# Identity matmuls in TensorE's waits, routing weights applied at the evictions, a rearranged last stage and swapped PSUM bank pairs, in a one-layer attention, retention and mixture-of-experts kernel

## What is computed

```python
mix = jnp.einsum('bse,ed->bsd', mixed, w_out)                    # mixed: 512 x 1024
h_res = h_res + gate1 * _rms_norm(mix, g_post_mix)
h2 = _rms_norm(h_res, g_pre_ffn) * (1.0 + scale2) + shift2
# router: 4 groups, best one; 8 experts in it, best two
g_prob = softmax(t @ w_group + b_group);  g_top, g_sel = top_k(g_prob, 1)
e_top, e_sel = top_k(softmax(e_logits of that group), 2)
weights = g_top * e_top / sum(e_top)
for e in range(32):
    hid = silu(t @ w_gate_exp[e]) * (t @ w_up_exp[e])            # 512 x 256
    y = y + combine[:, e:e + 1] * (hid @ w_down_exp[e])          # combine: weights at the chosen experts
h_res = h_res + gate2 * _rms_norm(y, g_post_ffn)
```

## Time and profile before

| what | value |
|---|---|
| median of 3 timed runs | 758.62 us (758.47 to 759.87) |
| the profiled execution | 759.44 us, span 757.4 us |
| PE busy | 640.0 us (85% of the span) |
| PE weight loads | 322.0 us (43%) |
| DVE busy | 375.3 us (50%) |
| ACT busy | 156.6 us (21%) |
| POOL busy | 79.6 us (11%) |
| mean granted TensorE clock | 0.937 of full speed |
| DMA | 171.75 MB, mean 227 GB/s |

### The profile page before, as it was taken

How to read it: one execution, slowest core, us unless ns; L and a number is a source line. 1 busy time by engine, 2 the same in 40 slices (tenths; PEclk the granted TensorE clock), 3 DMA queues, 4 the chain that set the end, 5 groups by cost and what they waited for, 6 DMA issues and landing times. The chain is left out here.

```text
span 757.4 us, 7042 instructions
## 1 busy us (share of the span) xinstructions
PE 640.0 (85%) x2446; PEld 322.0 (43%) x2446; DVE 375.3 (50%) x724; ACT 156.6 (21%) x333; POOL 79.6 (11%) x105
## 2 busy tenths in 40 slices
PE   0499999999999999999899954999786999979720
PEld 0465644444455555565544544334232444333200
DVE  5755356989876743258823247523121232212227
ACT  1420111233122222311222231022111122112112
POOL 0013211210111110000000001111111211200010
PEclk9999999999999999999999965999898999999975
DMA  9980806050506060430821093599999999999344
GB/s 327 384 325 15 298 20 223 17 206 7 216 1 222 1 223 0 170 89 0 332 112 56 28 391 154 213 419 419 421 422 420 421 404 386 419 419 417 138 169 169
DMA packets 50115, 171.75 MB, mean 227 GB/s; under 512 B 10016, under 2 KB 10016, under 8 KB 37152
## 3 DMA queue, kind: packets, MB, share of 16 engines
q1 hardware_dynamic: 41808, 154.98, 52.8%
q0 software_dynamic: 5888, 10.52, 3.7%
q10 hardware_dynamic: 2384, 5.80, 2.0%
HBM read 168.13 MB, written 13.63 MB: 240 GB/s over the span
## 5 line engine op out<-in xcount | busy, mean ns | idle before, releaser
L619 PE MATMUL psum<-ring,hT 128*128 128x512 f32 (+1 forms) x576 | 234.8, 561 | 0.0
L619 PEld LDWEIGHTS psum<-ring,hT 128*128 128x128 f32 x576 | 102.8, 191 | 119.3 <-issue 119.0
L869 PE MATMUL psum<-ring,hT 128*64 128x512 f32 (+1 forms) x416 | 127.1, 631 | 16.7 <-issue 16.7
L869 PEld LDWEIGHTS psum<-ring,hT 128*64 128x64 f32 (+1 forms) x416 | 43.2, 151 | 87.4 <-issue 87.3
L1551 DVE TENSOR_SCALAR work<-work 128x256 f32<-128x256 f32 x18 | 5.3, 294 | 137.2 <-PE psum L879 110.2
L895 PE MATMUL psum<-ring,work 128*64 128x512 f32 (+1 forms) x208 | 64.7, 626 | 8.4 <-issue 7.0
L753 PE MATMUL psum<-ring,hT 128*128 128x512 f32 x128 | 57.5, 608 | 2.7 <-DVE ring L1425 2.0
L1170 DVE SCALAR_TENSOR_TENSOR rows<-ring,sm,rows 128x512 f32<-128x512 f32 x64 | 51.1, 799 | 1.7
L869 PE MATMUL psum<-rows,hT 128*64 128x512 f32 (+1 forms) x96 | 42.5, 595 | 1.3 <-issue 1.3
L1077 ACT ACTIVATE work<-psum 128x256 f32<-128x256 f32 x18 | 6.9, 384 | 170.8 <-PE psum L869 170.8
L1230 DVE TENSOR_TENSOR ropebuf<-psum,cosT 128x512 f32<-128x512 f32 (+1 forms) x24 | 14.7, 614 | 51.6 <-PE psum L619 39.4
(11 more groups left out here) (240 smaller groups left out, 715.7 us busy)
## 6 DMA issues: line engine op xcount, KB each, us to landing
ring<-in_w_gate_exp SPq DMA_DIRECT2D x26, 1024.0 KB, 13.0
ring<-in_w_up_exp SPq DMA_DIRECT2D x26, 1024.0 KB, 20.4
ring<-in_w_down_exp SPq DMA_DIRECT2D x26, 1024.0 KB, 21.9
ring<-in_w_in SPq DMA_DIRECT2D x8, 2048.0 KB, 9.3
ring<-in_w_ada SPq DMA_DIRECT2D x8, 2048.0 KB, 14.3
ring<-in_w_ada SPq DMA_DIRECT2D x8, 1024.0 KB, 14.0
rows<-in_w_gate_exp SPq DMA_DIRECT2D x6, 1024.0 KB, 14.6
rows<-in_w_up_exp SPq DMA_DIRECT2D x6, 1024.0 KB, 21.3
```

The source lines that it names most:

```text
L619: mm = pe.matmul(o[:, 0:width], hT3[:, k, b * P:(b + 1) * P], w[:, k, :], start=(k == 0), stop=(k == KD - 1))
L869: mm = pe.matmul(o[rows, :], XT[u % 2][:, k, rows], both(SLOT_OF[place])[:, k, :, :], start=(k == 0), stop=(k == KD - 1))
```

## The change

Four things. (1) The bank pairs of `wout` are swapped: blocks 0 and 2 use banks 6 and 7, blocks 1 and 3 banks 0 and 1. (2) PE gets `stream(n)`, n matmuls of the identity with 512 columns of the constants into bank 6, which nobody reads: 3 behind `route(2)`, 6 behind `route(3)`, 3 behind the rank matmuls, 5 behind the first rows' table. (3) The routing weights go through the table of the late rows (`IN_WT`, 34 more columns) into `row_wt`, a column for each unit, and the evictions of the units multiply by it. (4) In the tail DVE adds the two rows, multiplies by G2 while ACT works, and ends with one instruction for reciprocal root and residual; ACT loads its square root's table ahead of `y_base`.

```diff
-            use(("wout", b), (0, 6)[b % 2], 2)
+            use(("wout", b), (6, 0)[b % 2], 2)
...
+            def stream(n):
+
+                o = ps[6]
+                for _ in range(n):
+                    pe.matmul(o[:, :], ident, cst[:, 0:512], start=True, stop=True)
...
                     if 2 <= b <= NB:
                         route(b - 2)
+                    if b == NB:
+                        pe.wait_ge(mix_n, NB - 1)
+                        stream(3)
                     if 1 <= b <= NB:
                         turn_h2(b - 1)
                 route(NB - 1)
+                stream(6)
...
+                stream(3)
                 pe.wait_ge(early_ready, 1)
...
                 mm.then_inc(early_done, 1)
+                stream(5)
...
-                    mm = pe.matmul(o[:, 0:NT], IN_ROW[:, n, :], IN_TILE[:, n, :], start=(n == 0),
+                    mm = pe.matmul(o[:, 0:2 * NT], IN_ROW[:, n, :], IN_BOTH[:, n, :, :], start=(n == 0),
...
-                a.activation(YO[u % 2][:, 0:512], ps[Y_BANK[(2 * u) % 3]][:, :], ACT.Copy).then_inc(y_evA, 1)
+                if u == 0:
+                    act.wait_ge(wt_ready, 1)
+                a.activation(YO[u % 2][:, 0:512], ps[Y_BANK[(2 * u) % 3]][:, :], ACT.Identity, bias=zero,
+                             scale=row_wt[:, u:u + 1]).then_inc(y_evA, 1)
...
+            a.activation(yr, eps.to_broadcast([P, NB]), ACT.Sqrt, bias=eps).then_inc(tail_root, 1)
+            act.wait_ge(tail_root, 1)
             act.wait_ge(y_base, 1)
...
-                v.tensor_tensor(wts[:, :, 1:2], wts[:, :, 0:1], P2, ALU.mult)
+                link(v.tensor_tensor(wts[:, :, 1:2], wts[:, :, 0:1], P2, ALU.mult))
...
+                v.tensor_tensor(IN_WT, IN_TILE, in_pairs(wts, NT), ALU.mult)
...
                 dve.wait_ge(table_done, 1)
+                v.tensor_copy(row_wt, bank(("table",))[:, NT:2 * NT]).then_inc(wt_ready, 1)
...
-                v.tensor_copy(YO[u % 2][:, 512:1024], ps[Y_BANK[(2 * u + 1) % 3]][:, :]).then_inc(y_evV, 1)
+                v.tensor_scalar(YO[u % 2][:, 512:1024], ps[Y_BANK[(2 * u + 1) % 3]][:, :], row_wt[:, u:u + 1], None,
+                                ALU.mult).then_inc(y_evV, 1)
...
+            def combine(b):
+                y = YG[b]
+                dve.wait_ge(y_back[b], 16)
+                relay(v.tensor_tensor(y[:, 0, :], y[:, 0, :], y[:, 1, :], ALU.add), y_sum, b + 1)
+
+            def weigh(b):
+                y = YG[b]
+                v.tensor_tensor(y[:, 1, :], y[:, 0, :], G2, ALU.mult)
+
+            def finish(b):
+                y = YG[b]
+                dve.wait_ge(y_sq, b + 1)
+                link(v.reciprocal(yss[:, b:b + 1], yr[:, b:b + 1]))
+                v.scalar_tensor_tensor(out=y[:, 1, :], in0=y[:, 1, :], scalar=yss[:, b:b + 1], in1=x3[:, b, :],
+                                       op0=ALU.mult, op1=ALU.add).then_inc(o_add, 1)
+
+            combine(0)
+            weigh(0)
+            for b in range(NB):
+                if b + 1 < NB:
+                    combine(b + 1)
+                finish(b)
+                if b + 1 < NB:
+                    weigh(b + 1)
```

More of the change, by code:

```diff
@@ L322, in build @@
         yss, yr = cols(238, 4), cols(242, 4)
+        over_wt = cols(246, 1)
         top8 = cols(248, 8)
@@ L365, in build @@
         y_out = [sem("y_out0"), sem("y_out1")]
-        yw_ready, y_ss, y_sq, o_add = sem("yw_ready"), sem("y_ss"), sem("y_sq"), sem("o_add")
+        y_ss, y_sq, o_add = sem("y_ss"), sem("y_sq"), sem("o_add")
         y_back = [sem(f"y_back{b}") for b in range(NB)]
@@ L379, in build @@
         y_base = sem("y_base")
+        wt_ready, y_sum, tail_root = sem("wt_ready"), sem("y_sum"), sem("tail_root")
         h2_dram = nc.dram_tensor("h2_rows", [S, D], F32, kind="Internal").ap()
@@ L524, in build @@
         IN_ROW = ropebuf[:, 0:2 * NB * P].rearrange("p (n c) -> p n c", n=2 * NB)
-        IN_TILE = ropebuf[:, 1024:1024 + 2 * NB * NT].rearrange("p (n t) -> p n t", n=2 * NB)
+        IN_BOTH = ropebuf[:, 1024:1024 + 4 * NB * NT].rearrange("p (n w t) -> p n w t", n=2 * NB, w=2)
+        IN_TILE, IN_WT = IN_BOTH[:, :, 0, :], IN_BOTH[:, :, 1, :]
+        row_wt = retbuf[:, 1408:1408 + NT]
         CUM = retbuf[:, 1344:1472].rearrange("p (b n) -> p b n", b=NB)
@@ L1113, in overflow @@
                 act.wait_ge(ov_y, o + 1)
-                a.activation(YO[0][:, 0:512], ps[6][:, :], ACT.Copy).then_inc(ov_evA, 1)
+                act.wait_ge(ov_ix, o * 3 + 3)
+                a.activation(YO[0][:, 0:512], ps[6][:, :], ACT.Identity, bias=zero, scale=over_wt).then_inc(ov_evA, 1)
             act.wait_ge(y_out[0], 16 * (NU // 2))
             each_overflow(act, overflow)
+            a.activation(yr, eps.to_broadcast([P, NB]), ACT.Sqrt, bias=eps).then_inc(tail_root, 1)
+            act.wait_ge(tail_root, 1)
             act.wait_ge(y_base, 1)
@@ L1123, in _ @@
             for b in range(NB):
-                act.wait_ge(yw_ready, b + 1)
+                act.wait_ge(y_sum, b + 1)
                 a.activation(JUNK2, YG[b][:, 0, :], ACT.Square, accum_out=yss[:, b:b + 1]).then_inc(y_ss, 1)
@@ L1581, in overflow @@
                 dve.wait_ge(ov_y, o + 1)
-                v.tensor_copy(YO[0][:, 512:1024], ps[7][:, :]).then_inc(ov_evV, 1)
+                dve.wait_ge(ov_ix, o * 3 + 3)
+                v.tensor_scalar(YO[0][:, 512:1024], ps[7][:, :], over_wt, None, ALU.mult).then_inc(ov_evV, 1)
             dve.wait_ge(y_out[0], 16 * (NU // 2))
             each_overflow(dve, overflow)
-            for b in range(NB + 1):
-                if b < NB:
-                    y = YG[b]
-                    dve.wait_ge(y_back[b], 16)
-                    link(v.tensor_scalar(y[:, 1, :], y[:, 1, :], wts[:, b, 1:2], None, ALU.mult))
-                    relay(v.scalar_tensor_tensor(out=y[:, 0, :], in0=y[:, 0, :], scalar=wts[:, b, 0:1], in1=y[:, 1, :],
-                                                 op0=ALU.mult, op1=ALU.add), yw_ready, b + 1)
-                if b >= 1:
-                    q, y = b - 1, YG[b - 1]
-                    dve.wait_ge(y_sq, q + 1)
-                    link(v.reciprocal(yss[:, q:q + 1], yr[:, q:q + 1]))
-                    link(v.scalar_tensor_tensor(out=y[:, 1, :], in0=y[:, 0, :], scalar=yss[:, q:q + 1], in1=G2,
-                                                op0=ALU.mult, op1=ALU.mult))
-                    v.tensor_tensor(y[:, 1, :], y[:, 1, :], x3[:, q, :], ALU.add).then_inc(o_add, 1)
+            def combine(b):
[19 more added lines that the diff above has]
+                    weigh(b + 1)
         @block.gpsimd
@@ L1677, in overflow @@
                 g.tensor_copy(six[:, :], pid_t[:, bass.ds(o + NU, 1)]).then_inc(ov_ix, 1)
-                pool.wait_ge(ov_ix, o * 2 + 2)
+                g.tensor_copy(over_wt, row_wt[:, bass.ds(o + NU, 1)]).then_inc(ov_ix, 1)
+                pool.wait_ge(ov_ix, o * 3 + 3)
                 pool.sem_inc(pool_steps, 1)
```

## The result

| what | before | after |
|---|---|---|
| median | 759.01 us (758.47 to 759.87, 4 runs) | 745.39 us (744.92 to 746.14, 4 runs) |
| the profiled execution | 759.44 us, span 757.4 | 745.19 us, span 743.1 |
| PE busy | 640.0 us | 648.0 us |
| DVE busy | 375.3 us | 373.3 us |
| ACT busy | 156.6 us | 160.1 us |

The ratio is 0.9818 (95% interval 0.9805 to 0.9831): 13.6 us faster. The forecast was 748.4, 11.0 under the profiled execution of before; the measured median lies 0.2 under the lower end of the range, 745.6.

A forecast was written before the change was run, and what follows sets the result against it. TensorE was taken to bound the kernel through the output projection, then a routing chain of alternating engines, then full DMA engines, then VectorE's tail. Sum: 759.44-3.7-3.5-3.9=748.3, stated as 748.4, range 745.6 to 752.0.

The forecast's parts named there:

- Part 1, bank pairs: Output projection: swapped banks end a wait and a half-clock stretch, second half starts near 379.3; 3.7 us, bounds 2.0 and 3.7.
- Part 2, routing chain: Chain between projection and expert stage: streams in TensorE's waits keep its clock up; 3.5 us, bounds 0 and 5.9.
- full list of cold terms: Routing chain through the first unit: what half clock costs TensorE's steps, cold rows against warm; 5.9 us all together.
- one more low stretch somewhere in the chain: Routing chain: deduction of 1.2 us for another spell of half clock, part of it falling into idle time.
- One for one: Expert stage, DMA full: it moves the same bytes whenever it starts, so gains before 481 us are kept at the end.
- Covered costs: Extra DVE work, late rows, wider table and scaled evictions: covered, taken as 0; evictions bounded at 0.1 on the very last.
- Part 3, tail: VectorE's tail after the expert stage: fewer and reordered steps save 3.9 us, bounds 3.2 and 4.1.
- the walk: VectorE's tail, instruction by instruction from 734.44: four finishes of 1.45, three multiplies and two adds of 1.25, ending at 750.3.
- The clock never falls: Rival on the routing chain: streams keep full clock throughout, the chain brings 5.9 us, time 746.0; chance 0.14.
- Transposes don't count: Rival on the routing chain: transposes don't hold the clock, so the chain brings 0.4 us, time 751.5; chance 0.15.
- The slower one: Rival on the routing chain: identity matmuls leave all four streams at half clock, overshooting by 11.9 us, time 763.7; chance 0.04.
- signs listed ahead: Whole kernel: clock falls near 437, router matmuls 2.0, first stream overshoots 1 us, expert loads near 473.8, VectorE's tail 15.9.

The follow-up runs named there:

- experiments 5: The changed kernel without the four streams and with the old bank pairs, leaving the weights at the evictions and the new tail; 755.22 us, ratio 0.9950.
- 2: The changed kernel without all four streams; 751.03 us, ratio 0.9898.
- 7: The changed kernel without its last two streams, behind the rank matmuls and behind the first rows' table; 747.95 us, ratio 0.9858.
- 11: The changed kernel with one streamed matmul ahead of the router matmuls of blocks 2 and 3, and the last stream cut from five to four; 746.09 us, ratio 0.9817.
- 12: The changed kernel measured again with more runs, nothing edited; 745.33 us, ratio 0.9818.
- experiment 3: The changed kernel with every streamed 512-column matmul replaced by six 128x128 transposes; 745.36 us, ratio 0.9827.
- experiment 6: The changed kernel with six matmuls instead of three in the first stream; 748.14 us, ratio 0.9868.
- experiment 9: The changed kernel plus three streamed matmuls ahead of the last unit and one ahead of the router matmuls of blocks 2 and 3; 746.28 us, ratio 0.9833.

## Why the prediction was right or wrong

The mechanisms were right in all three parts, and the gain came out too small: 11.0 us forecast, 13.6 by the medians, 14.3 by the profiled executions. Of the 3.2 missing in the profiles, 1.7 are the clock of the last unit, which stood in no term of the sum; 1.0 is the chain, where a deduction was too large; and 0.65 is the tail; the smaller terms take 0.1 off again.

**Part 1, bank pairs: right.** The half started at 369.18 and took 7.03, the second half at 379.50 (forecast 369.2, 7.0, 379.3). Against the profile 3.65 came, 3.7 was forecast; by the medians it is 2.7 alone, 2.9 in the changed kernel and 4.2 between experiments 5 and 2. The prediction's remark that the 0.8 between profile and median may be this stretch fits, but isn't shown.

**Part 2, routing chain: 4.5 instead of 3.5.** The full list of cold terms came to 5.9, and 1.2 was taken off for the first stream's overshoot at half clock: right in place and nearly in size (the stream ended 1.2 us after h2, and the path lost 1.0). The step that failed is "I take off 1.2 for one more low stretch somewhere in the chain". The stretch came, but it fell under the fourth stream, whose gap had slack; only 0.4 of it reached the path. It cost only what it slowed on the path, and here it slowed a stream, not the chain's own steps. By the prediction's terms with that corrected: 5.9-1.0-0.4=4.5, as measured.

**The expert stage: right, but the last unit is not part of it.** "One for one" held to 0.2 us in this kernel; in all fourteen profiles the stage took 225.1 to 226.1, against 225.4 in before. What failed is the unstated step behind it, that nothing after it changes but the tail. The last unit's matmuls come when the loads are done, and their clock was half for 3.4 us in before and full here: 1.7 us, in no term of the sum. The profiles show it at either clock from version to version (experiments 2, 7 and 11 against 12).

**Covered costs: right.** The evictions rose from 0.60 to 0.78 us on ACT and from 0.69 to 0.75 on DVE and cost 0.1 at the very end, the upper bound given. PE's wider table took 2.00 us, against 1.97.

**Part 3, tail: 4.55 instead of 3.9**, over its upper bound of 4.1. The order of the steps was right. First a slip: the walk ends at 750.3, and 754.33 less that is 4.0, not the 3.9 that went into the sum. The other 0.5 went wrong at "three multiplies and two adds of 1.25, steps included", and at four finishes of 1.45: an instruction of DVE that doesn't need its predecessor's result started about 0.1 before that one's end (728.67 and 1.28 make 729.95, the next starts at 729.87; 729.87 and 1.22 make 731.09, the next starts at 731.01). The trace of before has it too: the add at 740.92 ends at 742.15, and the next L1591 starts at 742.06. From reciprocal to reciprocal a block takes 3.79 us (728.47 to 732.26), not 1.45 and twice 1.25, 3.95. The bound of 4.1 rested on steps without such an overlap and so was none.

**The rivals.** "The clock never falls" was wrong on the clock (it fell twice) and came nearest in time, 746.0: luck, since its 1.4 us too many in the chain stand in for the last unit's 1.7. "Transposes don't count" fell with experiment 3. The slower one, all streams at half clock, did not come: the four took 4.52, 5.40, 2.82 and 6.24 us. Its rule that an overshoot is paid in full was right, as experiment 6 shows.

Of the signs listed ahead: the clock at 437, the router matmuls at 2.0, the overshoot of 1 us, no table load after `y_base` (715.11, before the loads at 719.89) came as told. The first loads of the expert stage went out at 473.01, not 473.8. The last stream ended 0.6 after its data, not before. VectorE's stretch was 15.34, not 15.9.

**What stays open.** What sets the last unit's clock. The start times don't sort the profiles: it began at 698.18 at full clock, at 697.87 (transposes) at half. Each version but the changed one has a single profile, so a difference between versions and one between executions of the same version can't be told apart by profiles; the two groups of times in experiment 11 would fit the latter, without showing it. The Trainium skill, "TensorE: Matmul & The Clock Gate", Part 1, says that the point where the clock changes varies from run to run of one kernel; the two profiles of the changed kernel don't show it (7.09 in both), the two groups of times would fit. That the streams are worth 5.6 us by the medians, and the chain only 4.5, speaks against the last unit's part being one execution's luck alone, but 1.1 is near what such medians can tell. And no version made the chain's further 0.9 to 1.3 us (experiments 3, 9, 11) count at the end: each lost as much or more at the last unit in its profile. A version with the two gaps filled and a shorter stream ahead of the last unit wasn't tried. None of the twelve measurably beats the changed kernel.

## What to carry to other kernels

Where a chain of small steps hands work between engines and TensorE's clock is seen to fall in it, price each of TensorE's steps there at both clocks from rows of the trace; filling its waits with work of no use can give back the difference (here 4.5 of 46.7 us), as long as each filler ends before the data comes: the overshoot of experiment 6 was paid one for one. Leave some slack in a gap where a low stretch may fall: under the fourth stream it cost only what stuck out, 0.4 us. And walk the program to its last instruction: a unit that follows a long stage with idle TensorE has a clock state of its own, and both states belong into the sum, or into its range.

## What the runs showed of the hardware

- f32 transposes of 128x128 hold the granted clock no worse than 512-column matmuls do: 1.00 over 455 to 465 with transposes in the gaps (experiment 3), 0.50 there with nothing in them (experiment 2).
- With one matmul of 512 columns in each of the two gaps of 0.79 us before the router matmuls of blocks 2 and 3, the clock stayed at 1.00 through 436 to 442 (experiment 9) and didn't fall at 437 in experiment 11 either. In all seven profiles with the same first stream, or twice it, of matmuls and without these two it fell between 435 and 440. Of the two only block 2's stands ahead of that place.
- The granted clock 230 us after the edited place differed from profile to profile: 7.09, 8.78 or 9.88 us for the same 32 records, 1.7 or 2.8 us on the path.
- On a 128x512 eviction from PSUM, ACT took 0.60 us for a Copy and 0.78 for an Identity with a column as bias and a column as scale; how the 0.18 divides between the two columns isn't shown. DVE took 0.69 for a copy and 0.75 for a multiplication by a column.
- Independent neighbours on DVE overlapped by about 0.08 us: the one at 728.67 takes 1.28, and the next begins at 729.87.
